# Eleven slots for expert weights instead of ten, in buffers paired by when they die

## What is computed

```
h = rmsnorm(x, g_mix);  proj = h @ w_in                 # lru_x, lru_gate, q, k, v, f, gate_lru, gate_fox
y_lru = rg_lru(conv(lru_x)) * gelu(lru_gate)            # branch A, width 1024
y_fox = forgetting_attention(q, k, v, cumsum(logf))     # branch B, 16 heads of 64
merged = sigmoid(gate_lru) * (y_lru @ w_lru_out) + sigmoid(gate_fox) * (y_fox @ w_fox_out)
x = x + merged @ w_o
h = rmsnorm(x, g_ffn)
logits = h @ w_router + b_router                        # 32 experts, top 4, softmax over the 4
for e in range(32):
    gu = h @ w_gate_up[e] + b_gate_up[e]                # 1024 -> 2048
    gate, up = min(gu[:, :1024], 7), clip(gu[:, 1024:], -7, 7)
    out += combine[:, e] * (((up + 1) * gate * sigmoid(1.702 * gate)) @ w_down[e] + b_down[e])
x = rmsnorm(x + out, g_final)
```

## Time and profile before

| | |
|---|---|
| median of 3 runs | 1251.7 us (1251.38 to 1252.92) |
| span of the profiled execution, first to last instruction | 1249.1 us |
| TensorE matmuls busy | 1170.3 us, 94% |
| DVE, ScalarE, GpSimd busy | 360.1, 254.1, 133.9 us |
| granted TensorE clock, mean | 0.990 |
| moved by DMA | 449.84 MB, mean 360 GB/s |
| pieces of expert weights | 192 of 2 MB (2.097 million bytes) |

### The profile page before, as it was taken

One profiled execution on the slowest core, in us unless ns is written; L12 is line 12 of the kernel. 1 busy time (PEld: TensorE's weight loads), 2 busy tenths in 40 slices (PEclk: granted clock), 3 DMA queues, 4 the chain that ended last, 5 costly groups with the idle time before them and its releaser, 6 DMA issues.

```text
span 1249.1 us, 14760 instructions
## 1 busy us (share of the span) xinstructions
PE 1170.3 (94%) x6454; PEld 612.9 (49%) x6454; DVE 360.1 (29%) x623; ACT 254.1 (20%) x411; POOL 133.9 (11%) x80
## 2 busy tenths in 40 slices
PE   4989999999999999999999899999999999999986
PEld 4989899999633333433333333333333333333321
DVE  5885978654310101111010101121110101010101
ACT  3445656634210000100000000001000001000002
POOL 5433332564000000000000000000000000000000
PEclk9989899999999999999999999999999999999999
DMA  9844344458999999999999999999999999999993
GB/s 249 283 136 136 114 157 136 140 176 318 429 427 426 427 429 428 428 427 427 428 427 428 428 427 428 427 429 427 428 427 427 428 427 427 428 428 427 427 427 162
DMA packets 73642, 449.84 MB, mean 360 GB/s; under 512 B 6876, under 2 KB 47912, under 8 KB 48872
## 3 DMA queue, kind: packets, MB, share of 16 engines
q1 hardware_dynamic: 72920, 447.03, 87.5%
q0 software_dynamic: 656, 1.84, 0.6%
HBM read 447.80 MB, written 1.05 MB: 359 GB/s over the span
## 4 chain that ended last, share of the span: by engine, by line
PE 58%; DMA 35%; ACT 2%; DVE 2%; issue 1%; POOL 1%; SPq 0%; DVEq 0%; ACTq 0%
DMA slot<-in_w_gate_up 34%; PE pj L1208 16%; PE pj L1053 16%; PE gb L1232 12%; PE gb L1195 3%; PE pt L1239 2%; PE s L1239 2%; PE pj L1220 1%; PE ga L1195 1%; ACT w_hi L457 1%; DMA mix<-in_w_in 1%; PE gb L1225 1%; PE s L1095 1%; PE pj L1201 1%; DVE w_lo L674 1%
## 5 line engine op out<-in xcount | busy, mean ns | idle before, releaser
L1208 PE MATMUL pj<-slot,GL 128*64 128x512 f32 x2048 | 455.7, 597 | 34.7 <-DMA slot<-in_w_gate_up 34.6
L1208 PEld LDWEIGHTS pj<-slot,GL 128*64 128x64 f32 x2048 | 141.3, 137 | 332.6 <-issue 263.1
L941 DVE TENSOR_SCALAR V<-pj 128x512 f32<-128x512 f32 x32 | 22.1, 692 | 736.4 <-PE pj L1208 736.4
L1232 PE MATMUL gb<-slot,V 128*64 128x512 f32 x1024 | 226.8, 595 | 0.0
L1053 PE MATMUL pj<-hT_hi,w_hi 128*128 128x256 f32 x448 | 130.7, 292 | 14.8 <-DVE hT_lo L679 8.5
L1232 PEld LDWEIGHTS gb<-slot,V 128*64 128x64 f32 x1024 | 70.7, 137 | 135.8 <-issue 135.8
L392 POOL TENSOR_TENSOR w_lo<-mix,w_hi 128x1024 fp32r<-128x1024 f32 x40 | 111.8, 2796 | 171.4 <-ACT w_hi L457 171.4
L1053 PE MATMUL pj<-hT_hi,w_lo 128*128 128x256 f32 x448 | 128.2, 286 | 0.0
L1053 PE MATMUL pj<-hT_lo,w_hi 128*128 128x256 f32 x448 | 128.2, 286 | 0.0
L581 ACT ACTIVATE V<-V 128x512 f32<-128x512 f32 x32 | 20.2, 630 | 518.8 <-DVE V L941 518.8
L421 POOL DMA_DIRECT2D slot<-in_g_final x1 | 0.6, 579 | 913.2 <-PE pj L1208 913.2
(11 more groups left out here) (278 smaller groups left out, 1062.7 us busy)
## 6 DMA issues: line engine op xcount, KB each, us to landing
slot<-in_w_gate_up SPq DMA_DIRECT2D x128, 2048.0 KB, 41.3
slot<-in_w_down SPq DMA_DIRECT2D x63, 2048.0 KB, 43.0
mix<-in_w_in SPq DMA_DIRECT2D x28, 1024.0 KB, 6.1
mix<-in_w_lru_out SPq DMA_DIRECT2D x4, 1024.0 KB, 5.1
mix<-in_w_fox_out SPq DMA_DIRECT2D x4, 1024.0 KB, 5.6
mix<-in_w_o SPq DMA_DIRECT2D x4, 1024.0 KB, 5.0
slot<-in_w_down SPq DMA_DIRECT2D x2, 1024.0 KB, 45.1
x_sb<-in_x SPq DMA_DIRECT2D x2, 512.0 KB, 4.4
```

The costliest lines, as they stand in the source:

```text
L941: v.tensor_scalar(gate, pj[0][:, :], LIMIT, None, ALU.min).then_inc(gate_ready, 1)
L1208: last = mm(pj[q // 2][h:h + SLOTS, :], hg[:, c, i, :], w[:, q * 512:(q + 1) * 512], start=False, stop=(c == GU_CHUNKS - 1))
L1232: last = mm(gb[h:h + SLOTS, :], actT[:, f % 4, f // 4, :], w[:, a * D + q * 512:a * D + (q + 1) * 512], start=False, stop=(f == KT - 1))
```

## The change

The 8 KB buffers are laid out anew, so that those which die at about the same time lie side by side and one slot of 16 KB covers both: K with LG, Q with V, hT_lo with XC, lru_pad with a buffer of its own that nothing else uses, hT_hi (later x2) with x_sb. There are 11 slots. The slab grows by 8 KB a partition, and Y, the router's small tiles, tri and ones get room of their own; the room that is held back for the DMA descriptors that GpSimd's software writes is set to 4 KB a partition (default 16 KB). What lay over Q and V in the expert stage (`h2T`, `gate`, `sig`, `up`, `actT`) lies over `x_sb`; `bgu_part` lies over GL, and DVE waits for `bgu_split` before it writes `pos`, which shares that room. Piece 0 is loaded ahead of the wait and the load of chunk 36; the other pieces follow behind chunk 39. `END_SLOT` becomes `EXP_PIECES` = 6.

```diff
-N_SLOTS = 10
+N_SLOTS = 11
+SCRATCH = 4096
...
-        slab_bytes = 23 * BUF + PADDED
+        slab_bytes = 24 * BUF + PADDED
...
-        lg_at, x_at = take(), take()
+        k_at, lg_at = take(), take()
+        q_at, v_at = take(), take()
+        hl_at, xc_at = take(), take()
+        lp_at, _ = take(PADDED), take()
+        hh_at, x_at = take(), take()
         x_sb = alias("x_sb", [P, TT, D], F32, x_at)
-        k_at, hl_at = take(), take()
-        hh_at = take()
...
-        slot_at = [mix_at[0], mix_at[2], k_at, mix_at[4], xc_at, mix_at[6], whi_at[0], r_at, whi_at[1], lg_at]
+        slot_at = [k_at, q_at, mix_at[0], mix_at[2], hl_at, lp_at, mix_at[4], mix_at[6], whi_at[0], r_at, whi_at[1]]
...
-        END_SLOT = N_SLOTS - 1
+        END_SLOT = EXP_PIECES
...
-        h2T = Q
+        def h2T_at(k):
+            return x_sb[:, k % 2, k // 2 * S:(k // 2 + 1) * S]
...
-        bgu_part = alias("bgu_part", [P, 1024], F32R, v_at + 4 * 1024)
+        bgu_part = alias("bgu_part", [P, 1024], F32R, gl_at + 4 * 1024)
...
-        gate = flat(V)[:, 0:512]
+        gate = flat(x_sb)[:, 0:512]
...
-        Y = alias("Y", [P, 512], F32, q_at)[:, :]
+        Y = sb("Y", [P, 512])[:, :]
...
+            free_after[k_at] = lambda: (sp.wait_ge(s_psum, HEADS), sp.wait_ge(ylru_ready, 1))
+            free_after[q_at] = lambda: (sp.wait_ge(o_psum, HEADS), sp.wait_ge(o_hi_ready, 2), sp.wait_ge(o_lo_ready, 2))
+            free_after[hl_at] = lambda: (sp.wait_ge(chunk_done, C_WF + 4), sp.wait_ge(m_lo_ready, 4))
+            free_after[lp_at] = lambda: sp.wait_ge(merged_ready, 4)
+            free_after[whi_at[0]] = lambda: sp.wait_ge(chunk_done, MIX_CHUNKS - 1)
+            free_after[r_at] = free_after[whi_at[1]] = lambda: sp.wait_ge(chunk_done, MIX_CHUNKS)
+
+            def load_expert_piece(q):
+                s = SLOT_OF[q]
+                if USER_BEFORE[q] is None:
+                    free_after[slot_at[s]]()
+                else:
+                    sp.wait_ge(chunk_done, MIX_CHUNKS + 2 * USER_BEFORE[q] + 2)
+                (load_piece if q + 1 < ALL_PIECES else load_last_piece)(q // EXP_PIECES, q % EXP_PIECES, s)
...
+                if c == C_WO:
+                    load_expert_piece(0)
                 if c >= MIX_RING:
                     sp.wait_ge(lo_dve_ready, c - MIX_RING + 1)
...
+            for q in range(1, ALL_PIECES):
+                load_expert_piece(q)
...
-                    act.activation(h2T[:, 2 * c:2 * c + 2, :].rearrange("p a b -> p (a b)"), acc[c // 2][c % 2][:, :],
+                    act.activation(x_sb[:, :, c * CC:(c + 1) * CC], acc[c // 2][c % 2][:, :].rearrange("p (a b) -> p a b", a=2),
...
+            dve.wait_ge(bgu_split, 1)
             dve.wait_ge(pos_psum, 1)
...
-    nc = bacc.Bacc("TRN2", target_bir_lowering=False, num_devices=1)
+    nc = bacc.Bacc("TRN2", target_bir_lowering=False, num_devices=1, dynamic_dma_scratch_size=SCRATCH)
```

More of the change, by code:

```diff
@@ L96, in hybrid_block @@
         w_lo = [alias(f"w_lo{i}", [P, KT, CC], F32R, at) for i, at in enumerate(wlo_at)]
-        lg_at, x_at = take(), take()
+        k_at, lg_at = take(), take()
[3 more added lines that the diff above has]
+        hh_at, x_at = take(), take()
         x_sb = alias("x_sb", [P, TT, D], F32, x_at)
-        k_at, hl_at = take(), take()
-        hh_at = take()
         hT_hi = alias("hT_hi", [P, KT, S], F32R, hh_at)
         hT_lo = alias("hT_lo", [P, KT, S], F32R, hl_at)
-        xc_at, lp_at = take(), take(PADDED)
         lru_pad = alias("lru_pad", [P, KT, S + CONV - 1], F32, lp_at)
@@ L111, in hybrid_block @@
         LG = alias("LG", [P, KT, S], F32, lg_at)
-        q_at = take()
         Q = alias("Q", [P, KT, S], F32, q_at)
         K = alias("K", [P, KT, S], F32, k_at)
-        v_at = take()
         V = alias("V", [P, TT, D], F32, v_at)
@@ L183, in hybrid_block @@
         junk = slot[END_SLOT][:, D:D + 512]
-        gate = flat(V)[:, 0:512]
-        sig = flat(V)[:, 512:1024]
-        up = flat(V)[:, 1024:1536]
-        actT = flat(V)[:, 1536:2048].rearrange("p (j h s) -> p j h s", h=2, s=SLOTS)
-        Y = alias("Y", [P, 512], F32, q_at)[:, :]
+        gate = flat(x_sb)[:, 0:512]
+        sig = flat(x_sb)[:, 512:1024]
+        up = flat(x_sb)[:, 1024:1536]
+        actT = flat(x_sb)[:, 1536:2048].rearrange("p (j h s) -> p j h s", h=2, s=SLOTS)
+        Y = sb("Y", [P, 512])[:, :]
         hg = flat(GL)[:, 0:1024].rearrange("p (k i s) -> p k i s", k=KT, i=2)
@@ L195, in hybrid_block @@
         EW = N_EXP + TOP_K
[L196 to L202, removed]
+        lg, rep, top8, msk, expw = (sb(n, [P, TT, w]) for n, w in (("lg", EW), ("rep", EW), ("top8", 8), ("msk", N_EXP), ("expw", N_EXP)))
+        tri, ones = sb("tri", [P, P])[:, :], sb("ones", [P, P])[:, :]
         comb = flat(GL)[:, 1920:1920 + TT * N_EXP].rearrange("p (t e) -> p t e", t=TT)
@@ L284, in _ @@
             sp.dma_start(rows[8:40, :], conv_w.rearrange("w (j p) -> (w j) p", p=P)).then_inc(rows_loaded, 16)
[L285 to L298, removed]
             def piece_src(e, m):
@@ L329, in _ @@
                 (load_piece if q + 1 < ALL_PIECES else load_last_piece)(q // EXP_PIECES, q % EXP_PIECES, s)
+            for c in range(MIX_CHUNKS):
+                if c == 2:
+                    sp.wait_ge(f_zeroed, 2)
+                    for r0 in (0, F_REST):
+                        sp.dma_start(wf[:, :, r0:r0 + HEADS], w_in[:, F_COL:F_COL + HEADS].rearrange("(k p) n -> p k n", p=P)).then_inc(small_loaded, 16)
+                        sp.dma_start(bf[r0:r0 + HEADS, :], b_f.rearrange("(h a) -> h a", a=1)).then_inc(small_loaded, 16)
+                    sp.dma_start(wr[:, :, :].rearrange("p (m i) n -> p m (i n)", i=2),
+                                 w_router.rearrange("(m p i) n -> p m (i n)", p=P, i=2)).then_inc(small_loaded, 16)
+                    sp.dma_start(brt[:, :], b_router.rearrange("(a n) -> a n", a=1).broadcast_to([P, N_EXP])).then_inc(small_loaded, 16)
+                if c == C_WO:
+                    load_expert_piece(0)
+                if c >= MIX_RING:
+                    sp.wait_ge(lo_dve_ready, c - MIX_RING + 1)
+                    sp.wait_ge(lo_pool_ready, c - MIX_RING + 1)
+                sp.dma_start(mix[c % MIX_RING].rearrange("p (k n) -> p k n", k=KT),
+                             mixer_chunk_src(c)).then_inc(mix_loaded[c % MIX_RING], 16)
+            for q in range(1, ALL_PIECES):
+                load_expert_piece(q)
             sp.wait_ge(flag_ready, 1)
@@ L852, in _ @@
             dve.wait_ge(h2T_psum, 4)
-            v.tensor_copy(h2T[:, 6:8, :].rearrange("p a b -> p (a b)"), acc[1][1][:, :]).then_inc(h2T_last, 1)
+            v.tensor_copy(x_sb[:, :, 3 * CC:], acc[1][1][:, :].rearrange("p (a b) -> p a b", a=2)).then_inc(h2T_last, 1)
             dve.wait_ge(sumsq2, 8)
@@ L869, in _ @@
                 link(v.match_replace(rep[:, t, :], top8[:, t, :], lg[:, t, :], -BIG))
-            v.tensor_tensor(msk, rep[:, :, TOP_K:], lg[:, :, TOP_K:], ALU.not_equal).then_inc(mask_ready, 1)
+            v.tensor_tensor(msk[:, :, :], rep[:, :, TOP_K:], lg[:, :, TOP_K:], ALU.not_equal).then_inc(mask_ready, 1)
             v.tensor_scalar(stat[:, 30:32], top8[:, :, TOP_K], -1.0, None, ALU.mult).then_inc(neg_top, 1)
             dve.wait_ge(mask_ready, 1)
+            dve.wait_ge(bgu_split, 1)
             dve.wait_ge(pos_psum, 1)
             link(v.scalar_tensor_tensor(pos[:, :, :], ga[:, 256:256 + TT * N_EXP].rearrange("p (t e) -> p t e", t=TT),
-                                        1.0, msk, ALU.add, ALU.mult))
+                                        1.0, msk[:, :, :], ALU.add, ALU.mult))
             def combine_weights():
                 dve.wait_ge(exp_top, TT)
-                link(v.tensor_tensor(expw, expw, msk, ALU.mult))
-                link(v.reduce_sum(stat[:, 32:34], expw, AX.X))
+                link(v.tensor_tensor(expw[:, :, :], expw[:, :, :], msk[:, :, :], ALU.mult))
+                link(v.reduce_sum(stat[:, 32:34], expw[:, :, :], AX.X))
                 link(v.reciprocal(stat[:, 34:36], stat[:, 32:34]))
-                v.tensor_tensor(comb, expw, stat[:, 34:36].unsqueeze(2).broadcast_to([P, TT, N_EXP]), ALU.mult).then_inc(comb_ready, 1)
+                v.tensor_tensor(comb, expw[:, :, :], stat[:, 34:36].unsqueeze(2).broadcast_to([P, TT, N_EXP]), ALU.mult).then_inc(comb_ready, 1)
                 dve.wait_ge(comb_ready, 1)
@@ L1144, in route @@
                 for k in (2 * c, 2 * c + 1):
-                    last = mm((ga, gb)[t][:, 0:N_EXP], h2T[:, k, t * P:(t + 1) * P], wr[:, k, :], start=(k == 0),
+                    last = mm((ga, gb)[t][:, 0:N_EXP], h2T_at(k)[:, t * P:(t + 1) * P], wr[:, k, :], start=(k == 0),
                               stop=(k == KT - 1))
```

4 lines of the change are left out of this document (removed).

## The result

The changed kernel takes 1244.91 us in the median of four runs (1244.46 to 1245.85), the kernel before 1251.54 us beside it: a ratio of 0.9950, interval 0.9938 to 0.9963. The forecast was 1246.9 us, 1244.6 to 1249.3. The profiled execution has a span of 1243.5 us, 5.6 us less than the one before.

What follows compares the result with a forecast made beforehand. The prediction took the expert stage's weight stream, 4.935 us a piece, as the bound. A 6.0 us larger lead less 1.2 us for g_final gave -4.8 us: 1251.7 to 1246.9 us, range 1244.6 to 1249.3.

Steps and rivals of the forecast that it cites:

- The bound and the sum: Expert stage: the weight stream sets the end, by pieces landed once it never stops, plus 4.935 us for each left.
- The lead: At the first free slot, eleven pieces landed against 9.83 before; 5.8 us gained by that count, 6.0 taken.
- The second reading of the lead: Counting back from piece 81 at 688.23 us to 330.8 us: 9.6 pieces landed before, so a gain of 6.9 us.
- The margin at expert 0's down matmuls: Next slot freed at 348.09 us, piece 15 good with 0.8 us to spare; costed at nothing, 1 us at most.
- g_final: Its 0.52 MB load now goes ahead of piece 189 and delays it by 1.2 us; bounds 0 to 2.1.
- The edits at no cost: DVE's added wait, moved buffers, chunk 36 sharing with piece 0, and the smaller descriptor room were to cost nothing.
- expert 0 not at 325.6: Sign of being wrong: expert 0 starting on TensorE at a time other than 325.6 us.
- The tail: The 28 us behind the last gate-and-up piece's release, near 1216.4 us, were to stay unchanged.
- Rival 1: More comes back: 6.9 us with g_final free, 1244.8 us, or 6.0 with it free, 1245.7; chance 0.14.
- Rival 2: Almost nothing comes back: late pieces, later first free slot or slower stream lose the lead; 1249.2 to 1252 us; chance 0.12.
- Rival 3: Slower: the smaller descriptor room holds up GpSimd's bias loads by some 9 us, giving 1256 us; chance 0.06.
- Rival 4: Piece 0's wait is late and its issue falls behind chunk 36; result still the forecast's; chance 0.02.

Runs made afterwards that it cites:

- e1: The changed kernel with ten slots instead of eleven, the new order and early loads kept: 1248.15 us, ratio 0.9973 to the kernel before.
- e2: The changed kernel with eleven slots but no piece loaded ahead of chunk 36, first load at 266 us as before: 1246.19 us, ratio 0.9958.
- e7: The kernel before with only the room for GpSimd's software descriptors set to 4 KB: 1251.54 us, ratio 1.0010.
- e5: The changed kernel with 16 more small matmuls ahead of the first gather, which delay expert 0: 1248.00 us, ratio 0.9976 to the kernel before.
- e3: The changed kernel with the load of g_final waiting until piece 189 has been used instead of piece 182: 1243.15 us, ratio 0.9928.
- e10: The changed kernel with g_final loaded after piece 189 and pieces 11, 12 and 15 loaded in halves: 1240.86 us, ratio 0.9916.
- e11: The changed kernel with g_final loaded after piece 189 and 8 small matmuls filling TensorE's gap in the tail: 1241.64 us, ratio 0.9924.
- e6: The kernel before with 16 more small matmuls ahead of the first gather, which delay expert 0: 1252.43 us, ratio 1.0012.
- e8: The changed kernel unchanged, timed and profiled a second time: 1244.85 us, ratio 0.9953 to the kernel before.
- e4: The changed kernel with pieces 11, 12 and 15 each loaded in two 1 MB halves as slot halves come free: 1244.00 us, ratio 0.9935.
- e9: The changed kernel with 8 small matmuls between expert 31's gate-and-up matmuls and its transposes: 1244.06 us, ratio 0.9941.

## Why the prediction was right

**The bound and the sum.** Right. The stream runs at 427 GB/s behind the hole and the pace is (1214.02 - 799.81) / 84 = 4.931 us a piece (105 to 189), forecast 4.935. The hole is as forecast too: from 325 to 360 us the engines moved 395 GB/s where 427.5 are the full rate, which is 2.7 us of stream missing; the prediction's terms with the slot free at 327.9 us give 327.9 + 1.6 - 326.8 = 2.7.

**The lead.** Right in its mechanism, too small in its size: 6.0 forecast, 7.0 us measured at pieces 105, 117, 129, 153, 165 and 177 (6.95 to 7.04 counted from the filler; 8.2 at 93 and 141, see the last section). e1 shows that the room makes 5.0 us of it. The other 2.0 come from the part of a piece by which the old ten slots were not full; e2 lays 1.0 to 2.3 us to the early starts. The term that was mis-sized is the time of the first free slot, 329.22 us, which I took "as now". That profile had TensorE's clock at half just before expert 0. The kernel before does not notice that 1.1 us (e7), the changed one counts on it 1 for 1 (e5). With the slot free at 327.9 us, which is 328.1 on the scale of the kernel before, and 1.6 us of restart, it has 9.51 + 0.5 x 0.4275 / 2.097 = 9.61 pieces in, and 1.39 x 4.93 = 6.9 us. The second reading of the lead, 6.9 us from the far end, came out nearer, but by luck: it counts back to the same moment, and with 329.7 us for 330.8 its own sum gives 1.65 x 4.935 = 8.1 us.

**The margin at expert 0's down matmuls** (0 to 1 us): nothing lost; the rate is 426 to 436 GB/s from 345 to 355 us.

**g_final.** Right in its cost: 1.2 forecast, 1.0 to 1.3 measured (e3, e10, e11). But at piece 189 it is hidden by something the prediction did not know: there the kernel before has just had one of its uneven steps of 1.2 us and the changed one has not. By lead and g_final alone the release would be 5.7 to 6.0 us earlier, and it is 7.0. That is luck of the piece at which the program ends. It was issued at 1182.46 us, forecast 1184. The DMA view of the changed kernel from 1170 to 1200 us (KB each, median us to landing):

```profile
slot<-in_w_down SPq DMA_DIRECT2D x1, 2048.0 KB, 48.8
slot<-in_w_down SPq DMA_DIRECT2D x2, 1024.0 KB, 46.8
slot<-in_g_final POOLq DMA_DIRECT2D x1, 512.0 KB, 10.7
```

The pieces issued just before it take 47 to 49 us, it lands in 10.7: it does not stand behind them. The Trainium skill (DMA: Bandwidth & Descriptors, Queues, rings and completion order) says that each engine takes a packet in turn from every queue with work; the trace agrees.

**The edits at no cost.** Right as far as the runs show: the smaller descriptor room (e7), the early loads (the w_o loads are issued at 233.46 us as before). Expert 0 starts 8.77 us behind the filler, 8.75 in e7 without the change. It starts at 324.22 us, and "expert 0 not at 325.6" was named as a sign of being wrong: it did tell of the mis-sized term above.

**The tail.** "Unchanged" was wrong in the profiled execution: 29.5 us, because the clock falls to half at 1221 us. It took back 1.6 of the 7.2 us. Whether the change has a part in it is open: e6, in the old layout, has the fall too, and e1, e2, e3 and e10 in the new one do not.

**Sum.** -7.2 + 1.6 = -5.6 us by span, forecast -4.8. By time -6.6 in the first comparison and -5.9 in the second (e8), so the carry-over from span to time is good to a microsecond only. The 2.6 us carried over set one execution's span against the median of other runs; where the record gives both for one execution, its time is 1.7 to 2.2 us above its span.

**The rivals.** Rival 1 (more comes back) had the lead right and g_final wrong. The time that it names, 1244.8 us, is the one measured, 1244.91, so the time alone would have spoken for it; only e3, e10 and e11 tell the two apart. Rival 2 named what would matter, the time of the first free slot, but with the wrong sign: it came earlier, not later. Rival 3 (GpSimd held up) is out by e7 and by the 2.15 us. Rival 4 did not occur.

## What to carry to other kernels

Where a stream of weights bounds the second stage, the gain of one more buffer is one buffer's transfer time at most, and it is cut to (slots - what has landed when the first slot is free again); starting the loads earlier is worth only what was missing to fill the room (some 2 of 7 us here), since the stream stands still once it is full. Check what then takes over: here the release of the first slot, which had 1 us to spare (2 without the fall of the clock) and now has none. And a small load on another queue that is moved ahead of the last piece cost its full transfer time here (1.0 to 1.3 us for 0.52 MB), although nothing waits for it.

## What the runs showed that was not expected

- TensorE's clock falls from 2.4 to 1.2 GHz for 3 to 4 us in some executions only: at 315 to 319 us (0.50; before and e6, not e7 and none of the new layout) and some 7 to 12 us behind the release of piece 189 (changed, e4, e5, e6, e8; not before, e1, e2, e3, e7, e10). Ahead of the later one TensorE had stood idle for 2 us, in the profiles with the fall and in those without it (e9 and e11 apart, where the gap is filled). It cost 1.1 us ahead of expert 0 and 1.6 us in the tail.
- The stream is not quite even: twelve pieces take 58.7 to 59.1 us three times and 59.9 to 60.1 once, in turn, in the kernel before (81 to 93, 129 to 141, 177 to 189) and one step later in the changed one (93 to 105, 141 to 153; its 60.0 from 177 to 189 are g_final, as e3 shows). So piece 189 is behind such a step in the kernel before and ahead of it in the changed one, which gave back the 1.2 us of g_final at that very piece. e6, the kernel before with nothing but a delay of 3.3 us, has its steps where the changed kernel has them, so they are not tied to the number of slots. In e2 and e4 they are spread over two stretches. What they are is open, and a release compared at one piece only can be wrong by 1.2 us for them.
- With eleven slots SP's own issues of 2 MB loads last up to 6.9 us (with ten: 1.8 us at most before and in e7, 2.4 in e1 and 3.2 in e6, but for the very last with 3.4 to 4.1). Nothing waits behind them but the next load, and the stream did not thin out.
